# Moving columns and weights an odd number of 64 bytes apart, and the mixers of two layers merged with their projection units

## The chip, the cores and the metric

The kernel runs on one core of one Trainium2 chip. The metric is the time of one execution in microseconds on the device; lower is better. Times of before and after are medians of several runs, and one more execution is recorded by the hardware profiler.

## The reference, cut to what matters

Two stacks of layers work on one sequence of 256 tokens with 1,024 channels, in float32.

```python
def first_block(x, c, ...):                    # 2 layers
    for l in range(DEPTH):
        mod = silu(c) @ ada_w[l] + ada_b[l]    # nine vectors of shift, scale, gate
        x = x + 0.5 * gt1 * swiglu(modulate(rmsnorm(x), sh1, sc1), ffn1_w_in, ffn1_w_out)
        x = x + gt2 * mixed(...)               # attention + convolution + gated linear attention
        x = x + 0.5 * gt3 * swiglu(modulate(rmsnorm(x), sh3, sc3), ffn2_w_in, ffn2_w_out)

def second_block(x, mem, ...):                 # 4 layers
    mem_n = rmsnorm(mem, norm_mem)
    for i in range(4):
        hn = rmsnorm(x, norm_mix[i])
        mix = (diff_attention, hgrn2, chunked_sgu)[i % 3](hn, ...)
        x = x + mix
        x = x + mem_cross_attention(rmsnorm(x), mem_n, w_q, w_kv, w_o)
        x = x + swiglu(rmsnorm(x), w_gu, w_down)
    return rmsnorm(x, norm_final)

def hgrn2(h, w_in, w_out, lb, onorm_g):        # layer 1 of the second block
    q, f, i, g = split(h @ w_in, 4)
    log_f = logaddexp(log(lb), log1p(-lb) + log_sigmoid(f)); key = 1 - exp(log_f)
    # per head: o[t] = sum over s <= t of (q[t] * product of exp(log_f) over (s, t]) . key[s] * i[s]
    return (rmsnorm(o, onorm_g) * silu(g)) @ w_out

def chunked_sgu(h, w_in, w_out, vnorm_g, w_s, b_s):   # layer 2
    u, v = split(gelu(h @ w_in), 2); v = rmsnorm(v, vnorm_g)
    mixed = tril(w_s) @ v per chunk of 128 tokens and group of 128 channels, + b_s
    return (u * mixed) @ w_out
```

Layers 0 and 3 of the second block have difference attention. The memory that cross-attention reads has 256 rows.

## The kernel before, in words

**Weights.** All weights are float32 in HBM (528 MB are read in all), and those of the projections stream through four slots of the tile `raw` (128 partitions x 2,048 floats each) on SP's DMA queue. A piece that fills a slot is a unit: 256 columns of a matrix with 1,024 rows, as eight tiles of 128 rows (k). ACT rounds a unit to the type fp32r into the slot's place in `whi` (L729), and DVE writes the remainder, `raw` less `whi`, into `wlo` (L1119). Activations are kept as two parts in the same way: `hhi` and `hlo` (the normed x, by columns of 256 tokens for each k), `mhi` and `mlo` (the normed memory), `ghi` and `glo` (the feed-forward product), and `fhi` and `flo` (the two halves of `parts_f`). A product is then three matmuls in fp32r, high by high, low by high and high by low, so a unit is 8 x 2 x 3 = 48 matmuls of 256 columns on TensorE (PE). `ahead(pos)` is the call by which ACT and DVE split the weights of coming units; a unit's result lies in one PSUM bank (`u.b`), which ACT or DVE evicts.

**Orders of the matmuls.** Their functions differ in what lies between two of them:

- `product` (L1790 to L1792): for each block m of 128 output columns, for each k, the three parts; also used by `half`, one m at a time.
- token-major units (L1836 to L1838, halves L2160 to L2162): the activation is the stationary operand and the weights are the moving one.
- `both` (L1808), for units that read h, and the output stage `outp` (L2314): for each k, part by part, both m.
- `ab_wide` (L1960, L1961) in the feed-forward stages of the second block: one matmul moves 512 columns (`fhi` and `flo` of one k) past `whi`, and one of 256 moves `fhi` past `wlo`. A unit has 16 such pairs; there are 88 such units.
- `outs` (L1975, in the last step L2015): the output weights of the feed-forward stages, with `ghi` and `glo` moving, 24 matmuls per slot and step of 128 output rows.

A feed-forward step is three units' worth of work, 144 matmuls of 256 columns where it is not wide. In three of the four feed-forward stages of the first block the modulation's matrix (`ada_w`) is also loaded and multiplied.

**Addresses.** Each partition of SBUF holds the tiles one behind the other, in the order of the `sb(...)` calls. Before, a step of `PHASE` = 8 floats (32 bytes) is added behind each slot of `whi` and `wlo` and in front of each of `hlo`, `mhi`, `mlo`, `ghi`, `glo` and `parts_f`. Taken modulo 32 floats and relative to `whi`, slot s of `whi` and `wlo` begins at 8 s, `hhi` at 0, `hlo` at 8, `mhi` at 16, `mlo` at 24, `ghi` at 0, `glo` at 8, and `fhi` and `flo` at 16. An odd number of 64 bytes is 16 floats modulo 32.

**Layers with hgrn and sgu.** The order of work is that of the list `stages`, which every engine's program runs through; each engine works strictly in that order, and semaphores (`q[...]`, `read`, `used`) order engines against one another. Layer 1 has a stage `project` (12 units hq, hf, hv), a stage `tree8` (a tree of nine levels over the tokens: per level PE multiplies keys and queries of all eight heads, 32 matmuls of 128x128, L2044, DVE scales queries and keys for the next level, L1453 and L1454, and copies the level's part of the matrix out of PSUM, L1478), and a stage `hgrn_out` (4 gate units, the sums over tokens, the norm, the product with the gate). Layer 2 has `project` (4 units su, 4 units sv), then `sgu`: transposed spatial weights, the norm of v, mixed matmuls (L2269), the product with u. In both, memory's values (units xv) are projected later, ahead of cross-attention. The difference attention of layers 0 and 3 is already one stage, in which its units are laid among the heads (`DIFF_ORDER`, the first five of them, `LEAD`, ahead). Its own units take PSUM banks 0 and 1 in turn, and memory's values too. The two key units of cross-attention (xk) come ahead of the mixer's norm and take the next banks of the running count; ACT evicts them (L879). In layer 3 the banks are those of the first own units, in layer 0 they are others.

## Time and profile before

| | |
|---|---|
| median of 3 runs | 2966.79 us (2960.71 to 2968.15) |
| profiled execution | 2968.39 us, span of the records 2966.6 us |
| PE busy | 2796.0 us, 94% of the span, 21,031 matmuls |
| DVE, ACT busy | 1951.2 us (66%), 1368.4 us (46%) |
| read from HBM | 528.10 MB, 179 GB/s over the span |
| mean clock granted to PE | 0.972 of full speed |

Busy times come from the records of one execution. The record of a matmul reaches over the start of the next ones, so a mean record of 280 ns doesn't say that a matmul takes 280 ns of the engine; the time from one start to the next does. "Idle before" is the time for which an engine stood still ahead of an instruction of the group, and behind the arrow stands what ended it; "issue" is time for which the profile shows no reason. The mean clock below 1 comes from stretches in which PE has little to do.

### The profile page before, as it was taken

The page shows a single profiled execution, that of the slowest core. Times are in us where ns is not written, and L with a number is a line of the kernel's source. Part 1 is how long each engine was busy: PE and PEld are TensorE (multiplying, and loading weights), DVE is VectorE, ACT ScalarE, POOL GpSimd, SP SyncE. Part 2 cuts the span into 40 slices and gives each one's busy share as a digit, 9 for nine tenths or more (in the row PEclk, how much of TensorE's full clock was granted, in tenths as well). Part 3 has the DMA queues.
Part 4 walks back from the last instruction along what each step waited for, and adds up shares of the span by engine and source line. Part 5 has one row for each costly group of instructions (what it writes and reads, how often), then busy time and mean ns, then how long its engine had stood idle before and what let it go on. Part 6 is the DMA issues. An engine that isn't in the chain of part 4 may idle for free.

```text
span 2966.6 us, 50727 instructions
## 1 busy us (share of the span) xinstructions
PE 2796.0 (94%) x21031; PEld 2655.9 (90%) x21031; DVE 1951.2 (66%) x2718; ACT 1368.4 (46%) x1640; POOL 0.7 (0%) x5
## 2 busy tenths in 40 slices
PE   6899979999998899999999978999989999999998
PEld 5899869999998699999899978999989899999897
DVE  5887776878777655676566665566655566675665
ACT  3335434344354354555454514454544544554453
POOL 0000000000000000000000000000000000000000
PEclk8899979999999899999999999999999999999999
DMA  8987506868864145655255623445645255543453
GB/s 238 323 283 239 173 13 236 294 234 293 291 227 148 43 162 178 203 167 170 90 195 185 213 72 108 134 143 197 198 157 185 97 201 192 190 143 115 170 177 107
DMA packets 458799, 533.02 MB, mean 180 GB/s; under 512 B 9879, under 2 KB 435081, under 8 KB 458633
## 3 DMA queue, kind: packets, MB, share of 16 engines
q1 hardware_dynamic: 457340, 530.11, 53.8%
q8 instruction: 109, 1.79, 0.3%
q10 hardware_dynamic: 1293, 0.65, 0.1%
q14 instruction: 57, 0.47, 0.0%
HBM read 528.10 MB, written 2.62 MB: 179 GB/s over the span
## 4 chain that ended last, share of the span: by engine, by line
PE 85%; DVE 8%; ACT 2%; issue 2%; DMA 1%; SPq 0%; ACTq 0%; DVEq 0%
PE ps L1975 15%; PE ps L1960 11%; PE ps L1808 10%; PE ps L2314 8%; PE ps L1790 7%; PE ps L1791 6%; PE ps L1792 6%; PE ps L1961 6%; PE ps L2044 2%; PE ps L2015 2%; DVE wlo L1119 2%; DVE work L1499 1%; PE ps L1838 1%; PE ps L1836 1%; PE ps L1837 1%
## 5 line engine op out<-in xcount | busy, mean ns | idle before, releaser
L1119 DVE TENSOR_TENSOR wlo<-raw,whi 128x2048 fp32r<-128x2048 f32 (+1 forms) x514 | 976.4, 1918 | 424.9 <-ACT whi L729 421.2
L729 ACT ACTIVATE whi<-raw 128x2048 fp32r<-128x2048 f32 (+1 forms) x514 | 826.6, 1615 | 388.5 <-PE ps L1792 119.7
L1960 PE MATMUL ps<-parts_f,whi 128*128 128x512 f32 x1408 | 499.5, 397 | 10.2 <-issue 10.2
L1790 PE MATMUL ps<-hhi,whi 128*128 128x256 f32 x1488 | 426.3, 286 | 15.7 <-issue 13.0
L1791 PE MATMUL ps<-hlo,whi 128*128 128x256 f32 x1488 | 421.7, 283 | 0.0
L1792 PE MATMUL ps<-hhi,wlo 128*128 128x256 f32 x1488 | 421.6, 283 | 0.0
L1961 PE MATMUL ps<-parts_f,wlo 128*128 128x256 f32 x1408 | 397.0, 282 | 0.0
L1975 PE MATMUL ps<-glo,whi 128*128 128x256 f32 x1280 | 360.7, 282 | 0.0
L1975 PE MATMUL ps<-ghi,whi 128*128 128x256 f32 x1280 | 358.8, 280 | 1.6 <-DVE wlo L1119 1.5
L1975 PE MATMUL ps<-ghi,wlo 128*128 128x256 f32 x1280 | 359.6, 281 | 0.0
L1960 PEld LDWEIGHTS ps<-parts_f,whi 128*128 128x128 f32 x1408 | 267.2, 190 | 70.9 <-issue 11.6
L1790 PEld LDWEIGHTS ps<-hhi,whi 128*128 128x128 f32 x1488 | 283.6, 191 | 19.7 <-issue 19.6
L1791 PEld LDWEIGHTS ps<-hlo,whi 128*128 128x128 f32 x1488 | 284.3, 191 | 0.5 <-issue 0.5
L1792 PEld LDWEIGHTS ps<-hhi,wlo 128*128 128x128 f32 x1488 | 284.1, 191 | 0.0
L1961 PEld LDWEIGHTS ps<-parts_f,wlo 128*128 128x128 f32 x1408 | 267.0, 190 | 0.1
L1975 PEld LDWEIGHTS ps<-ghi,whi 128*128 128x128 f32 x1280 | 241.9, 189 | 3.8 <-issue 2.2
L1975 PEld LDWEIGHTS ps<-ghi,wlo 128*128 128x128 f32 x1280 | 240.7, 188 | 0.0
L1975 PEld LDWEIGHTS ps<-glo,whi 128*128 128x128 f32 x1280 | 240.6, 188 | 0.0
L1808 PE MATMUL ps<-hhi,whi 128*128 128x256 f32 x992 | 206.1, 290 | 20.1 <-DVE hlo L1284 16.2
L1808 PE MATMUL ps<-hlo,whi 128*128 128x256 f32 x992 | 201.4, 285 | 0.0
L1808 PE MATMUL ps<-hhi,wlo 128*128 128x256 f32 x992 | 201.3, 285 | 0.0
L1223 DVE SCALAR_TENSOR_TENSOR work<-work,silu_c 128x256 f32<-128x256 f32 x490 | 196.9, 476 | 0.0
(275 smaller groups left out, 4684.9 us busy)
## 6 DMA issues: line engine op xcount, KB each, us to landing
raw<-in_ffn_w_in SPq DMA_DIRECT2D x88, 1024.0 KB, 7.9
raw<-in_ffn_w_gu SPq DMA_DIRECT2D x88, 1024.0 KB, 5.1
work<-in_ada_w SPq DMA_DIRECT2D x72, 1024.0 KB, 8.2
raw<-in_ffn_w_out SPq DMA_DIRECT2D x88, 512.0 KB, 5.9
raw<-in_ffn_w_down SPq DMA_DIRECT2D x88, 512.0 KB, 5.6
raw<-in_ca_w_kv SPq DMA_DIRECT2D x32, 1024.0 KB, 5.7
raw<-in_mix_w_in SPq DMA_DIRECT2D x24, 1024.0 KB, 6.2
raw<-in_da_w_in SPq DMA_DIRECT2D x24, 1024.0 KB, 5.3
```

The lines of the kernel that those rows point to most:

```text
L729: f(whi[:, s, 0:size], raw[:, s, 0:size], ACT.Copy).then_inc(hi_done[s], 1)
L1119: tt(wlo[:, s, 0:size], raw[:, s, 0:size], whi[:, s, 0:size].bitcast(F32), ALU.subtract).then_inc(lo_done[s], 1)
L1223: m = stt(acc, w, silu_c[:, k:k + 1], acc, ALU.mult, ALU.add)
L1790: mm(dst, wh, xh, start=first, stop=False)
L1791: mm(dst, wh, xl, start=False, stop=False)
L1792: return mm(dst, wl, xh, start=False, stop=last)
L1808: o = mm(ps[:, slot, 256 * m:256 * m + 256], w[:, k, P * m:P * m + P], x_[:, k, :], start=k == 0 and i == 0 and m == 0, stop=k == KT - 1 a ...
L1960: mm(ps[:, banks[m], :], th[:, k, c], parts_f[:, :, k, :], start=k == 0, stop=False)
L1961: o = mm(ps[:, banks[m], 0:S], tl[:, k, c], fhi[:, k, :], start=False, stop=k == KT - 1)
L1975: o = mm(dst, a_, b_[:, t, :], start=first and t == 0 and i == 0 and m % 2 == 0, stop=False, skip_group_check=True)
L2015: o = mm(dst, a_, b_[:, t, :], start=False, stop=t == 1 and i == 2 and m % 2 == 1, skip_group_check=True)
L2314: o = mm(ps[:, bank, 256 * m:256 * m + 256], w[:, k, P * m:P * m + P], x_[:, k, :], start=k == 0 and i == 0 and m == 0, stop=k == KT - 1 a ...
```

## The change

The memory's layout, the two stages of layers 1 and 2, and the choice of banks change; the arithmetic is the same.

1. **Layout.** The steps of 8 floats are gone. `Slots` puts slot s of `whi` and `wlo` at 2,048 s + 32 (s // 2) floats. 48 floats stand ahead of `hhi`, 32 ahead of `mhi`, nothing between the others. Modulo 32 floats, all slots of `whi` and `wlo` are at 0 and all moving tensors at 16.
2. **hgrn.** One stage of 20 units in place of three stages: the 16 of before and memory's values. Five lead. The tree is cut in two half trees of four heads, one after the other, 18 half levels of 16 matmuls; behind each half level 1 or 2 halves of a unit follow (`H_FILL`), behind the last eight more. The sums over tokens, norms and gate products of the first half tree's heads are laid among the second's levels. `hv` is evicted by ACT, before by DVE. The result goes to `fhi` and `flo`, before to `hhi` and `hlo`.
3. **sgu.** One stage of 12 units: su 0, sv 0 to 3, su 1 to 3, memory's values. The spatial weights are turned behind the third, the four mixed steps stand behind units 6 to 9 (from 0). The result goes to `fhi` and `flo`.
4. **Banks.** `banks_beside(keys)` gives the first own units of the diff and hgrn stages the two banks of 0 to 3 that the key units don't use; after that two banks alternate. `st.reads` is taken behind the units, where before it was taken ahead of them.

```diff
-PHASE = 8
+class Slots:
+    def __getitem__(self, key):
+        rows, s, cols = key
+        at = UNIT * s + 32 * (s // 2)
+        return self.v[rows, at + cols.start:at + cols.stop]
...
+    def banks_beside(self, keys):
+        beside = sorted({0, 1, 2, 3} - {u.b for u in keys}, reverse=True)
+        first = 1 - beside[1] if beside[1] < 2 else 0
+        return chain(beside, cycle((first, 1 - first)))
...
-        whi = sb("whi", [P, SLOTS, UNIT + PHASE], F32R)
-        wlo = sb("wlo", [P, SLOTS, UNIT + PHASE], F32R)
+        whi = Slots(sb("whi", [P, SLOTS * UNIT + 32], F32R))
+        wlo = Slots(sb("wlo", [P, SLOTS * UNIT + 32], F32R))
         x = sb("x", [P, KT, S])
+        sb("phase_h", [P, 48])
         hhi = sb("hhi", [P, KT, S], F32R)
-        sb("phase_hlo", [P, PHASE])
         hlo = sb("hlo", [P, KT, S], F32R)
-        sb("phase_mhi", [P, PHASE])
+        sb("phase_m", [P, 32])
         mhi = sb("mhi", [P, KT, S], F32R)
-        sb("phase_mlo", [P, PHASE])
         mlo = sb("mlo", [P, KT, S], F32R)
-        sb("phase_ghi", [P, PHASE])
         ghi = sb("ghi", [P, 2, S], F32R)
-        sb("phase_glo", [P, PHASE])
         glo = sb("glo", [P, 2, S], F32R)
-        sb("phase_parts_f", [P, PHASE])
         parts_f = sb("parts_f", [P, 2, KT, S], F32R)
...
+        HGRN_ORDER = (("hq", 0, 0), ("hq", 0, 1), ("hf", 1, 0), ("hf", 1, 1), ("hq", 0, 2),
+                      ("hq", 0, 3), ("hf", 1, 2), ("hf", 1, 3), ("hv", 2, 0), ("hv", 2, 1), ("hv", 2, 2),
+                      ("hv", 2, 3), ("hgate", 3, 0), ("hgate", 3, 1), ("hgate", 3, 2), ("hxv", 4, 0),
+                      ("hgate", 3, 3), ("hxv", 4, 1), ("hxv", 4, 2), ("hxv", 4, 3))
+        H_FILL = (1, 1, 2, 1, 1, 2, 1, 1, 2, 1, 1, 1, 1, 1, 1, 1, 1, 2)
+        H_DONE = [LEAD - 1 + sum(H_FILL[:g]) // 2 for g in range(len(H_FILL) + 1)]
...
+                banks = plan.banks_beside(keys)
+                st.own = [plan.column(w, at * D, name, n, next(banks), token_major=at == 2)
+                          for name, at, n in DIFF_ORDER]
...
+        def half_tree(st, g):
+            side, L = divmod(g, LEVELS)
+            return st.tree + side, L, HALF * side
+        def half_bank(tree, h, L):
+            return 4 + 2 * ((LEVELS * tree + L) % 2) + h // 2
...
+            def hgrn(st):                       # VectorE
...
+                for g in range(2 * LEVELS):
+                    tree, L, h0 = half_tree(st, g)
...
+                    up(tree, L, hq[:, heads, :], hk[:, heads, :], hf[:, heads, :])
+                    if g:
+                        keep(g - 1)
+                        for m in range(H_DONE[g - 1], H_DONE[g]):
+                            evict(us[m + 1])
+                            ahead(us[m + 2].pos)
...
+            def sgu(st):                        # VectorE
+                for n in range(3):
+                    ahead(us[n].pos)
...
+                ahead(us[6].pos)
+                for p in range(4):
+                    ahead(us[7 + p].pos)
+                    gated(p)
+                ahead(us[11].pos)
...
+            def hgrn(st):                       # TensorE
...
+                for u, src in us[:LEAD]:
+                    unit(u, src, st.h)
+                for b in (2, 3):
+                    pe.wait_ge(read[b], st.reads[b])
+                for g, n in enumerate(H_FILL):
...
+                    pe.wait_ge(q["level_cp"], LEVELS * tree + L - 1)
+                    level(tree, L, hq, hk, HALF,
+                          lambda h, L: ps[:, half_bank(tree, h, L), 256 * (h % 2):256 * (h % 2) + 256],
+                          lambda h: (slice(0, P), h0 + h))
+                    if g == LEVELS + 2:
+                        tokens(0)
+                    if g == LEVELS + 4:
+                        pair_sum(0)
+                    if g == LEVELS + 6:
+                        tokens(1)
+                    if g == LEVELS + 8:
+                        pair_sum(1)
+                    fill(n)
+                fill(1)
+                tokens(2)
+                tokens(3)
+                fill(2)
+                pair_sum(2)
+                fill(1)
+                pair_sum(3)
+                fill(4)
...
+                for n, u in enumerate(us):      # TensorE, sgu
+                    unit(u, "h" if n < 8 else "mem", st.h)
+                    if n == 2:
+                        turn_weights()
+                    if 6 <= n <= 9:
+                        mixed(n - 6)
...
-                    hi, lo = (fhi, flo) if st.mixer.kind == "diff" else (hhi, hlo)
+                    hi, lo = (fhi, flo) if st.mixer.kind in ("diff", "hgrn", "sgu") else (hhi, hlo)
```

## Rows read from the trace of the kernel before

**Rows 1.** The page, the chain of work that ended last, by engine.
```profile
PE 85%; DVE 8%; ACT 2%; issue 2%; DMA 1%; SPq 0%; ACTq 0%; DVEq 0%
```

**Rows 2.** Windows over two feed-forward stages: length, busy us (records) of each engine, PE clock, DMA share, GB/s.
```profile
502.83:647.15 144.32, 144.32 (x1219) 144.32 (x1218) 113.94 (x177) 54.90 (x48) 0.00 (x0) 1.00 0.86 292
1085.48:1222.17 136.69, 136.69 (x1154) 136.69 (x1154) 68.00 (x66) 57.72 (x51) 0.00 (x0) 1.00 0.58 192
```

**Rows 3.** Groups of PE's matmuls by line, whole span: busy us, mean ns of a record, idle before.
```profile
L1960 PE MATMUL ps<-parts_f,whi 128*128 128x512 f32 x1408 | 499.5, 397 | 10.2 <-issue 10.2
L1790 PE MATMUL ps<-hhi,whi 128*128 128x256 f32 x1488 | 426.3, 286 | 15.7 <-issue 13.0 <-DVE wlo L1119 2.7
...
L1975 PE MATMUL ps<-glo,whi 128*128 128x256 f32 x1280 | 360.7, 282 | 0.0
...
L1808 PE MATMUL ps<-hlo,whi 128*128 128x256 f32 x992 | 201.4, 285 | 0.0
...
L2314 PE MATMUL ps<-hlo,whi 128*128 128x256 f32 x512 | 104.8, 287 | 0.0
...
L1836 PE MATMUL ps<-whi,hhi 128*128 128x256 f32 x256 | 74.0, 289 | 0.0
...
L2162 PE MATMUL ps<-whi,hlo 128*128 128x256 f32 x96 | 26.9, 280 | 0.0
```

**Rows 4.** Timeline of PE, output units of the difference-attention layers: start us, us, what.
```profile
1358.06 0.65 PE L2314 MATMUL ps<-parts_f,whi 128*128 128x256 f32 x4
...
1363.54 0.63 PE L2314 MATMUL ps<-parts_f,whi 128*128 128x256 f32 x4
...
1369.19 0.64 PE L2314 MATMUL ps<-parts_f,whi 128*128 128x256 f32 x4
...
2672.39 0.62 PE L2314 MATMUL ps<-parts_f,whi 128*128 128x256 f32 x4
...
2677.83 0.63 PE L2314 MATMUL ps<-parts_f,whi 128*128 128x256 f32 x4
```

**Rows 5.** Windows over a part of a mixing stage and over two neighbouring wide units (slots 0, 1).
```profile
320.00:370.00 50.00, 46.01 (x345) 41.62 (x343) 46.42 (x72) 25.37 (x26) 0.00 (x0) 0.98 0.46 148
2000.91:2006.54 5.63, 5.63 (x35) 4.93 (x34) 3.05 (x4) 1.58 (x2) 0.00 (x0) 1.00 0.85 298
2006.54:2012.08 5.54, 5.54 (x34) 4.87 (x33) 2.08 (x3) 3.04 (x3) 0.00 (x0) 1.00 0.26 104
```

**Rows 6.** Window over the hgrn tree and gate units.
```profile
1729.40:1829.50 100.10, 73.67 (x520) 69.23 (x519) 63.35 (x110) 21.12 (x26) 0.00 (x0) 0.91 0.17 53
```

**Rows 7.** Groups by line in that window: busy us, mean ns, idle before and releasers.
```profile
L2044 PE MATMUL ps<-work 128*128 128x128 f32 x256 | 35.1, 303 | 18.9 <-DVE work L1454 15.3 <-DVE work L1444 2.6 <-DVE work L1420 1.1
...
L1478 DVE COPY_PREDICATED work<-con,ps 128x256 f32<-128x256 int32 x56 | 19.3, 436 | 0.0
...
L1119 DVE TENSOR_TENSOR wlo<-raw,whi 128x2048 fp32r<-128x2048 f32 x4 | 9.2, 2288 | 7.0 <-ACT whi L729 7.0
L1453 DVE TENSOR_TENSOR work<-work 128x1024 f32<-128x1024 f32 x7 | 8.6, 1226 | 9.9 <-PE ps L2044 9.8
```

**Rows 8.** The chain in that window, one level of the tree: start us, us.
```profile
1745.04 3.82 PE ps L2044 x32
```

**Rows 9.** Window over the spatial gating's own work.
```profile
2194.90:2222.50 27.60, 18.45 (x134) 17.45 (x133) 14.91 (x22) 11.39 (x15) 0.00 (x0) 0.88 0.26 77
```

**Rows 10.** Timeline at the first unit of the last layer.
```profile
2546.61 0.99 DVE L1284 SCALAR_TENSOR_TENSOR hlo<-work,hhi 128x256 fp32r<-128x256 f32 x2
...
2547.88 0.77 PE L1808 MATMUL ps<-hhi,whi 128*128 128x256 f32 x2 [3.91 <-ACT work L879]
```

**Rows 11.** Window over that unit's first matmuls.
```profile
2547.80:2550.20 2.40, 2.32 (x11) 2.35 (x12) 0.74 (x1) 2.40 (x3) 0.00 (x0) 0.50 0.02 7
```

**Rows 12.** Timeline of PE, output weights in the feed-forward stage from 502 us.
```profile
502.67 0.28 PE L1975 MATMUL ps<-ghi,whi 128*128 128x256 f32 x1
...
505.59 0.28 PE L1975 MATMUL ps<-ghi,whi 128*128 128x256 f32 x1
```

More of the change, by code:

```diff
@@ L15 @@
 from contextlib import ExitStack
+from itertools import chain, cycle
 import numpy as np
@@ L451, in build @@
                 w = a["hg_w_in_2"][j]
-                units = project("hgrn", plan.columns(w, 0, 4, "hq") + plan.columns(w, D, 4, "hf")
-                                + plan.columns(w, 2 * D, 4, "hv", token_major=True))
-                tree = take("tree")
-                stages.append(Stage(kind="tree8", units=units, tree=tree))
-                gate = plan.columns(w, 3 * D, 4, "hgate")
-                last_use[0] = gate[-1]
-                stages.append(Stage(kind="hgrn_out", units=gate, last=gate[-1], tree=tree, gn=take("gn", 4)))
+                st = Stage(kind="hgrn", tree=take("tree", 2), gn=take("gn", 4))
+                banks = plan.banks_beside(keys)
+                st.own = [plan.column(*((w, at * D, name, n) if at < 4 else (wkv, D, name, n)), next(banks),
+                                      token_major=at in (2, 4)) for name, at, n in HGRN_ORDER]
+                st.reads = list(plan.reads)
+                st.units = st.own
+                st.by = {u.what: u for u in st.own}
+                last_use[0] = st.by["hgate", 3]
+                vunits = [st.by["hxv", n] for n in range(4)]
+                stages.append(st)
                 w_out = a["hg_w_out_2"][j]
@@ L461, in build @@
                 w = a["sg_w_in_2"][j]
-                units = project("sgu", plan.columns(w, 0, 4, "su") + plan.columns(w, D, 4, "sv", token_major=True))
-                stages.append(Stage(kind="sgu", units=units, last=units[-1]))
+                st = Stage(kind="sgu")
+                st.own = plan.columns(w, 0, 1, "su") + plan.columns(w, D, 4, "sv", token_major=True)
+                st.own += [plan.column(w, 0, "su", n, plan.slot) for n in (1, 2, 3)]
+                st.gates, st.inner = st.own[:1] + st.own[5:], st.own[1:5]
+                last_use[0] = st.own[-1]
+                st.mem = vunits = plan.columns(wkv, D, 4, "sxv", token_major=True)
+                st.units = st.own + st.mem
+                stages.append(st)
                 w_out = a["sg_w_out_2"][j]
@@ L477, in build @@
                                 pairs=take("pairs", 4)))
+            stages[-1].values = ([xv[:, :, 256 * h:256 * h + 256] for h in range(4)], h_xv, s_xv)[i % 3]
             ready = out_project(a["ca_w_o_2"][i])
@@ new lines, in next_unit @@
+                def next_unit(m):
+                    evict(us[m])
+                    ahead(us[m + 1].pos)
+                for u in us[:LEAD - 1]:
+                    take_out(u)
+                ahead(us[LEAD - 1].pos)
+                for m in range(LEAD - 1, 12):
+                    next_unit(m)
+                act.wait_ge(q["level_mm"], LEVELS * (st.tree + 1))
+                squares(0)
+                next_unit(12)
+                norm_root(0)
+                next_unit(13)
+                squares(1)
@@ new lines, in sgu, with next_unit, high @@
+            def sgu(st):
+                us = st.units
+                def next_unit(n):
+                    evict(us[n])
+                    ahead(us[n + 1].pos)
+                def high(p):
+                    act.wait_ge(q["sgu_v"], SG_V + 2 * p + 2)
+                    f(fhi[:, 2 * p:2 * p + 2, :], s_t[:, p % 2, :], ACT.Copy).then_inc(q["sgu_hi"], 1)
+                ahead(us[0].pos)
+                for n in range(5):
+                    next_unit(n)
+                log_exp_tables()
+                for w_, n in all_read(st.inner):
@@ L2108, in mix1 @@
                             pe.wait_ge(q["level_cp"], LEVELS * st.tree + j)
-                        level(st, j, c_q, c_k, 4, dst, part)
+                        level(st.tree, j, c_q, c_k, 4, dst, part)
                     if j == 4:
@@ L2233, in hgrn_out, with hgrn, fill, tokens @@
-            def hgrn_out(st):
-                us = st.units
-                pe.wait_ge(q["level_cp"], LEVELS * (st.tree + 1))
-                def tokens(pair):
-                    if pair > 1:
-                        pe.wait_ge(q["gn_out"], st.gn + pair - 1)
-                    for h in (2 * pair, 2 * pair + 1):
-                        o = over_tokens(ps[:, 4 + pair % 2, 256 * (h % 2):256 * (h % 2) + 256], hv,
+            def hgrn(st):
+                us = [(u, "mem" if u.what[0] == "hxv" else "h") for u in st.units]
+                values = [st.by["hv", p] for p in range(4)]
+                halves = iter([(u, src, m) for u, src in us[LEAD:] for m in range(2)])
+                def fill(n):
+                    for _ in range(n):
+                        half(*next(halves))
+                def tokens(p):
+                    pe.wait_ge(*bank_read(values[p]))
+                    pe.wait_ge(q["level_cp"], LEVELS * (st.tree + p // 2 + 1))
+                    if p == 1:
+                        pe.wait_ge(q["gn_out"], st.gn + 1)
+                    for h in (2 * p, 2 * p + 1):
+                        o = over_tokens(ps[:, (2, 2, 4, 6)[p], 256 * (h % 2):256 * (h % 2) + 256], hv,
```

263 lines of the change are left out of this document (143 added, 120 removed).

## The prediction

> **What bounds the kernel now.** I read the page first, and of it the chain of work that ended last. PE holds 85% of it, DVE 8%, DMA 1% [rows 1]. So a transfer made earlier is worth next to nothing, and two things are: the time PE takes for one matmul, and the places where it stands still. For the first, the windows over whole feed-forward stages: in the one from 1085 us PE is busy all of its 136.69 us and issues 1,152 of the 256-column matmuls (1,154 records; 8 steps of 144), so one every 118.6 ns, at full clock, with DMA at 0.58. In the stage from 502 us DMA is at 0.86 and DVE at 79%, and still PE is never idle: 144.32 us [rows 2]. Its busy records overlap (mean 280 to 290 ns each), so a matmul's price is the step from one start to the next, never the mean of a record. Then the groups of PE by line, for how many there are: L1790 to L1792 1,488 each, L1975 1,280 each of three, L1808 992 each, L2314 512 each, which make 12,816; twenty smaller groups (L1836 with 256 the first, L2162 with 96 the last) hold 3,360 more; and 1,408 pairs of a 512- and a 256-column matmul come from the wide units (L1960, L1961) [rows 3]. For the second, windows, groups and the timeline of the three stages that the edits touch [rows 6 to 12].
>
> **Part 1, the spacing of moving columns and weights.** It changes no instruction, only addresses. The trace of before has one stream in which every moving tensor already lies an odd number of 64 bytes from the weights that the array takes in beside it: the output units of the difference-attention layers whose weights are in slot 0 (fhi, flo at 16 floats modulo 32, whi and wlo of slot 0 at 0). The other three slots are 8, 16 and 24 floats on. The starts of these units' 48 matmuls tell the price: slot 0 takes 1363.54 − 1358.06 = 5.48 us, the next 1369.19 − 1363.54 = 5.65; in the last layer slot 0 takes 5.44 [rows 4], which is 113.3 ns a matmul and so 5.2 under the 118.5 that I take as the mean of all such units (the stage above gives 118.6). The first of the two begins at the old spacing and only then settles, at 0.04 us the unit.
>
> The layout after puts all four slots and all moving tensors in the position of that one stream. Which matmuls gain? Of 16,176, those of the two mixing stages of the first block stand behind DVE, which is busy 46.42 of 50 us there [rows 5]; I leave out their 26 units, 1,248, so 14,928 stay. 14,928 × 5.2 ns = **−78**; settling in half of the 311 units, 0.04 us each, **+6**. The bounds: nothing, if that stream is quick for another reason than its addresses (its order of matmuls is one of five in the kernel); or 0.0054 us each, −84, if the mean is taken from the stage and all settle at once.
>
> The wide units go the other way. The wide unit in slot 0 has odd multiples already (parts_f and slot 0) and takes 5.63 us; the one in slot 1, at 32 bytes, 5.54 [rows 5]. After, all 88 are like slot 0. If slots 1 and 3, half of them, go up by 0.09: **+4**; bounds 0 and +8 (all of them).
>
> The Trainium skill ("TensorE: Matmul & The Clock Gate", Part 2, the step on LDWEIGHTS) says that TensorE has two independent SBUF read ports and that "Loading the next tile's weights doesn't steal SBUF read bandwidth from the running matmul." By that, addresses could not matter, and the term would be 0. The trace disagrees as far as two slots of one stream differ by 3 to 4% with the same instructions [rows 4]; but it shows it for one stream alone, so the rule stays a rival below.
>
> **Part 2, hgrn in one stage.** Now the tree and the gate units take 100.10 us in which PE is busy 73.67 [rows 6]. A level is 32 matmuls in 3.82 us (0.119 each) [rows 8], then PE stands until DVE has done both products of the next level (L1453 and its like on L1454, 1.23 us each) [rows 7]. PE's own work by start steps: 4 gate units of 5.65, 22.6; 272 tree matmuls at 0.119, 32.4; 32 + 8 for tokens and sums, 32 × 0.12 + 8 × 0.24 = 5.8; 16 of the output unit, 1.9: 62.7. So 37 us are waits and half clock (the granted clock is 0.91). After, a half level is 16 matmuls (1.9 us), with one half unit (2.7) behind it in 14 of 18 levels and two in four. DVE has per half level: the two products at half size, a little over half of 1.23 each, 1.35; the small fold behind them, which I put at 0.3; four copies (L1478) at 0.44, 1.74; and 11 units' low halves (L1119) at 2.29 over 18 levels, 1.40: 4.8 us against PE's 1.9 + 22/18 × 2.7 = 5.2. PE is the longer on average, but in a level with one half unit a low half (2.29) in front of the products (1.7 with the fold) makes 4.0 against a cover of 2.7, 1.3 late; in half of the 14 such levels that is 9 us. The way in and out of the tree I put at 2. Gain 37 − 9 − 2 = **−26**; bounds −37 and, if every level is late by 1.5, 18 × 1.5 + 2 = 29, −8. The values of memory that come into this stage are the same units moved; hv's eviction goes from DVE to ACT, which is busy 21.12 of 100 us here. SP's queue gets the same transfers in the order of units; DMA is at 0.17 here, so that hides it.
>
> **Part 3, sgu among units.** 27.60 us, PE busy 18.45 [rows 9]: 9.2 idle. After, two units (11 us) lie between the last sv and the first mixed matmuls, and memory units behind each pair. The cover is a unit's 5.4 us per pair; DVE is busy 14.91 us in the whole stretch, under 3.8 for each of the four pairs even if all of it were theirs. **−9**, bounds −4.5 (half of it comes back as waits on ACT and DVE among the units) and −9.
>
> **Part 4, banks of the first units.** In the last layer PE waits 3.91 us for ACT's eviction of the keys from bank 0 (L879), which stands in order behind the norm on ACT; then the clock is 0.50 for the 2.40 us to 2550.20, which do half of their work, 1.2, and some more behind [rows 10, 11]. With another bank the units start as soon as the norm's first columns are there. **−6**, bounds −3.9 and −7. What is late next is the norm's last column: it is done at 2546.61 + 0.99 = 2547.60, and a unit begun at 2547.88 − 3.91 = 2543.97 wants it 7 × 0.68 = 4.8 later, at 2548.7. So it is not late.
>
> **Sum**, against the profiled execution, 2968.4 (span 2966.6 and 1.8 around it): 2968.4 − 78 + 6 + 4 − 26 − 9 − 6 = 2859.4. The median of the runs shown is 1.6 lower: **2858**.
>
> **The rivals.** Parts 2 to 4 alone are −41.
>
> A, the forecast: 0.47; its own range is 2835 to 2880: below by 6 (part 1 at −84), 6 (no settling) and 11 (tree at −37), above by 4 (wide at +8) and 18 (tree at −8).
>
> B, addresses do nothing on average: the stream of rows 4 is quick for its order and its place. For it: the trace has no other order at 113 ns, and the wide units are slower at that spacing. Against it: slot 1 of the same order, in the same stage, is slower. 2968.4 − 41 − 1.6 = 2926. It is also what the skill's rule of two ports would give. 0.22.
>
> C, only the order by two columns of weights for each k settles (L1808 with 2,976 and L2314 with 1,920 records, the order of the quick stream): 4,896 × 5.2 = 25; the orders of L1790, L1836 and L1975, which write one bank area until it is complete, keep their step. 2926 − 25 + 4 = 2905. 0.18.
>
> D, the forecast with a tree that gains nothing, each half level being late behind DVE's low halves and the copies: 2858 + 26 = 2884. 0.06; DVE's 4.8 against 5.2 is close.
>
> E, slower. The layout puts every unit where the worst reading of before is: the output weights of the stage at 502 us take 505.59 − 502.67 = 2.92 us for 24, 121.7 ns [rows 12]. That is 3.2 ns over the mean: 14,928 × 3.2 = +48, +4 for the wide, −41: 2968.4 + 11 − 1.6 = 2978. The sign turns where (41 − 4) / 14,928 = 2.5 ns are lost, at 121.0 ns a matmul. Against it: that unit's slot lies 8 floats from the quick position. 0.05.
>
> Some 0.02 are left for no net change, a loss of phases that eats the stages' 41.
>
> **How the numbers follow.** A measurement of this kernel tells about 0.3%, 9 us, from no change. A, B, C and D are faster, 0.93; 0.02 same and 0.05 slower, of which I move 0.01 to same for an E that is half as bad: 0.93, 0.03, 0.04. The likeliest is A: 2858. The range is to leave out 2 in 10: A's lower half reaches to 2835; above it must take in D, C and B, whose own spread is ± 5: up to 2932. That leaves E, the no change and the tails.
>
> **What would show it.** In the profile after: a plain feed-forward stage of eight steps like that from 1085 us at 8 × 144 × 113.3 ns = 130.5 us instead of 136.7 (B: 136.7 still; C: 136.7 there, while units of L1808 take 5.44 us; E: 140); every output unit (L2314) at 5.44 to 5.48 us in all four slots; wide units of all slots at 5.63. The hgrn tree with 18 levels at 5.2 us of PE, and idle time of L2044 for DVE under 10 us in place of 18.9; over 25 would be D. In sgu no idle time of PE over 1 us in front of the mixed matmuls; no wait for L879 in front of the first unit of the last layer. The prediction is wrong if the cause of the quick stream is not the distance of moving data from weights, if DVE's or ACT's operand reads slow as their own addresses move, or if the quick step only lasts for streams without a neighbour.

## The result, and the profile after

The kernel after takes 2872.46 us (median of 4 runs, 2870.35 to 2875.08); before takes 2967.38 (4 runs, 2960.71 to 2968.15). The ratio is 0.9685, 95% interval 0.9668 to 0.9702: 94.9 us quicker. The forecast was 2858, so 109 quicker. Five later runs of the same kernel gave 2873.47.

The page of the profiled execution (2870.35 us, span 2868.6), the chain of work that ended last, by engine. It answers to [rows 1]:

```profile
PE 83%; DVE 9%; ACT 3%; issue 3%; DMA 2%; SPq 1%; ACTq 0%; DVEq 0%
```

PE still holds the chain, with a little less of it: its matmuls have become shorter, the waits of the other engines mostly have not. Then windows over the stretches that answer to [rows 2, 5, 6, 9] (length, busy us and records of each engine, clock of PE, DMA share, GB/s): eight steps of the second and of the last feed-forward stage of the first block, the ten steps of its first one up to the last outputs, two wide units in one stage and two in the next, the merged hgrn stage from the tree's first level to its output, the merged sgu stage, and one token-major unit:

```profile
500.78:639.55 138.77, 138.77 (x1218) 138.77 (x1218) 112.09 (x176) 55.67 (x48) 0.00 (x0) 1.00 0.92 299
1066.37:1197.19 130.82, 130.82 (x1154) 130.82 (x1154) 68.01 (x66) 57.69 (x51) 0.00 (x0) 1.00 0.60 197
96.26:275.22 178.96, 170.63 (x1435) 169.99 (x1434) 149.18 (x254) 66.01 (x58) 0.00 (x0) 0.95 0.89 290
1461.25:1472.54 11.29, 11.29 (x67) 9.88 (x65) 6.91 (x7) 4.62 (x5) 0.00 (x0) 1.00 0.75 258
1937.53:1948.62 11.09, 11.09 (x66) 9.77 (x65) 5.23 (x7) 4.62 (x5) 0.00 (x0) 1.00 0.61 209
1662.72:1792.29 129.57, 121.76 (x996) 118.16 (x994) 89.31 (x149) 59.49 (x58) 0.00 (x0) 0.99 0.34 108
2077.16:2161.68 84.52, 83.58 (x718) 83.28 (x717) 57.18 (x57) 48.28 (x53) 0.00 (x0) 1.00 0.62 198
1232.84:1238.51 5.67, 5.67 (x51) 5.67 (x50) 4.37 (x2) 2.40 (x2) 0.00 (x0) 1.00 1.09 360
```

The reader is to see, line by line: the stage that took 136.69 us takes 130.82 (130.5 was forecast), with the same 1,152 matmuls, so 113.6 ns for each; the one with DMA at 0.86 took 144.32, takes 138.77 and has DMA at 0.92, still without an idle moment of PE. In the first feed-forward stage PE idles 8.3 us. A wide unit takes 11.29 / 2 = 5.65 us in the one stage and 5.55 in the other. The merged stages keep PE busy for 94 and 99% of their time. The last line is a unit of the token-major order: 5.67 us for 48 matmuls, no quicker than before (117.9 ns a matmul on average).

The timeline of PE at the first three output units of layer 0, and the start of the fourth (start us, us, what), answers to [rows 4]:

```profile
1332.53 0.71 PE L2472 MATMUL ps<-parts_f,whi 128*128 128x256 f32 x4 [0.99 <-DVE work L1507]
...
1338.13 0.62 PE L2472 MATMUL ps<-parts_f,whi 128*128 128x256 f32 x4
...
1343.57 0.62 PE L2472 MATMUL ps<-parts_f,whi 128*128 128x256 f32 x4
...
1349.01 0.62 PE L2472 MATMUL ps<-parts_f,whi 128*128 128x256 f32 x4
```

The second and third slot now take 5.44 us as the first did in the last layer before; the first one, 5.60, has a wait of 1 us in front and settles.

Where the time went, from the start of the first matmul of each stretch in the traces of four kernels (us; the two in the middle are the first two experiments):

| stretch | before | layout alone | structure alone | after |
|---|---|---|---|---|
| start, to the first output weights | 93.8 | 95.5 | 93.7 | 96.3 |
| first feed-forward stage | 183.5 | 184.4 | 183.0 | 186.2 |
| the other three of the first block | 517.7 | 496.7 | 517.6 | 496.9 |
| mixing stages and their outputs | 348.3 | 339.8 | 349.3 | 340.5 |
| layer 0, difference attention | 122.9 | 121.5 | 124.0 | 122.6 |
| layer 1, mixer to the end of cross-attention | 279.1 | 273.7 | 249.9 | 246.9 |
| layer 2, the same | 173.4 | 170.3 | 161.5 | 158.7 |
| layer 3, difference attention | 129.4 | 127.8 | 123.0 | 120.9 |
| four wide feed-forward stages | 658.9 | 650.9 | 658.9 | 650.4 |
| the rest, up to the last of these | 444.6 | 435.4 | 444.4 | 434.6 |
| sum | 2951.6 | 2895.9 | 2905.3 | 2853.7 |

### The profile page after: what moved, and what is told of

Its sections match the earlier page's. It is cut to its first block, busy times and chain, and to the rows that moved or that the text cites. A ratio compares the mean times of both kernels' runs of the same rounds, so it can differ in the third digit from the quotient of the medians.

```text
span 2868.6 us, 50786 instructions
## 1 busy us (share of the span) xinstructions
PE 2717.4 (95%) x21031; PEld 2579.0 (90%) x21031; DVE 1940.6 (68%) x2727; ACT 1389.5 (48%) x1664; POOL 0.7 (0%) x5
## 4 chain that ended last, share of the span: by engine, by line
PE 83%; DVE 9%; ACT 3%; issue 3%; DMA 2%; SPq 1%; ACTq 0%; DVEq 0%
PE ps L2097 14%; PE ps L2082 11%; PE ps L1930 9%; PE ps L2472 7%; PE ps L1912 7%; PE ps L1913 6%; PE ps L1914 6%; PE ps L2083 6%; DVE wlo L1206 2%; PE ps L2137 2%; DMA work<-in_ada_w 2%; DVE work L1586 2%; PE ps L2166 1%; PE ps L2282 1%; PE ps L2284 1%
## 5 line engine op out<-in xcount | busy, mean ns | idle before, releaser
L2082 PE MATMUL ps<-parts_f,whi 128*128 128x512 f32 x1408 | 497.7, 396 | 11.9 <-issue 11.9
L1912 PEld LDWEIGHTS ps<-hhi,whi 128*128 128x128 f32 x1600 | 303.7, 190 | 21.0 <-issue 21.0
L1913 PEld LDWEIGHTS ps<-hlo,whi 128*128 128x128 f32 x1600 | 303.8, 190 | 0.7 <-issue 0.7
L1914 PEld LDWEIGHTS ps<-hhi,wlo 128*128 128x128 f32 x1600 | 303.3, 190 | 0.0
```

The lines of the kernel that those rows point to most:

```text
L1912: mm(dst, wh, xh, start=first, stop=False)
L1913: mm(dst, wh, xl, start=False, stop=False)
L1914: return mm(dst, wl, xh, start=False, stop=last)
L2082: mm(ps[:, banks[m], :], th[:, k, c], parts_f[:, :, k, :], start=k == 0, stop=False)
```

## The experiments

Steps are given below as the time from one start to the next, 48 matmuls a unit, by unit from the traces. "Moving less whi" is the distance in floats of the tensor that moves from the slot's high part, modulo 64; in the kernel after it is 48 for h in slots 0 and 1 and 16 in slots 2 and 3, and the other way round for all other moving tensors. wlo lies 32 from whi. A unit is called quick if its mean step, past its first matmuls, is under 114.5 ns. Of `product`, the units that read h are counted (101, before 94); 16 more read the memory.

**Layout alone, structure alone.**

The first is the kernel before with this edit; the second is the kernel after with the same edit undone.

```diff
-        whi = sb("whi", [P, SLOTS, UNIT + PHASE], F32R)
-        wlo = sb("wlo", [P, SLOTS, UNIT + PHASE], F32R)
+        whi = Slots(sb("whi", [P, SLOTS * UNIT + 32], F32R))
+        wlo = Slots(sb("wlo", [P, SLOTS * UNIT + 32], F32R))
         x = sb("x", [P, KT, S])
+        sb("phase_h", [P, 48])
         hhi = sb("hhi", [P, KT, S], F32R)
-        sb("phase_hlo", [P, PHASE])
...
```

> The kernel before with the new addresses and nothing else. Theory 1 (addresses set the step of a matmul, and the parts add up): column-major units at 113.3 ns, token-major units at 117.8 as in the profile after, so about 13,800 matmuls outside the mixing stages gain 4 to 5 ns, less what the first feed-forward stage can't use because its transfers bound it: 55 to 65 us, 2902 to 2912. Theory 2 (the step came from something in the new order of work, as a busier PE): units stay at 118 to 119 ns, within 10 us of 2967.

> The kernel after with the addresses of before: merged hgrn and sgu stages and the choice of banks. Theory 1 (parts add up): what is left of 95 us when the addresses give 55 to 65, so 30 to 40 us under 2967, 2927 to 2937, and my sum of the three parts said 41. Theory 2: 2870 to 2880. First feed-forward stage of before, 183.5 us, without the two waits of 2.5 and 4.1 us for wlo. If those waits stay with the old addresses, they belong to the execution, not to the quicker PE.

Measured: 2914.79 (4 runs, ratio 0.9828, 0.9811 to 0.9845) and 2923.81 (0.9849, 0.9831 to 0.9867), beside 2967.66. So 52.9 and 43.8 us; their sum is 96.7, the whole change 94.9. The parts add up, and theory 1 holds, with the layout 2 us under and the structure 4 us over the gain that I gave as the nearest end. In the layout's run every group of column-major units goes from 117.4 to 119.0 ns on average to between 113.4 and 115.6, the 38 token-major units stay (117.9, 117.7), the wide pairs too (349.7, 350.1). The first feed-forward stage takes 183 to 186 us in all four kernels.

**The roles of the two positions.**

```diff
 raw = sb("raw", [P, SLOTS, UNIT])
+sb("phase_w", [P, 16])
 whi = Slots(sb("whi", [P, SLOTS * UNIT + 32], F32R))
...
-sb("phase_h", [P, 48])
+sb("phase_h", [P, 16])
```

> The kernel after with all of whi and wlo moved to 16 floats modulo 32 and all activations to 0: the same distances, the roles of the two positions exchanged. If only the distance counts: column-major units 113.3 ns, token-major ones 117.8, time 2870 to 2875. If it counts which position the stationary operand has (at 0 quick, at 16 slow): column-major units go to 117.8 (+60 us) and token-major ones to 113.3.

Measured: 2878.48 us, one run. Most column-major units stay at 113.3, token-major ones at 117.7: the position of either one doesn't count, the distance does. But this layout also turns each 48 into a 16 and back, and that shows. The wide pairs exchange: 353 ns in slots 0 and 1, 347 in 2 and 3. And of the units of `product` and the output weights, 68 of 101 and 110 of 160 are at 113.3, in the kernel after 95 of 101 and 148 of 159; the rest are near 119, all in slots where moving less whi is 16.

**No step between the slots.**

```diff
-        at = UNIT * s + 32 * (s // 2)
+        at = UNIT * s
```

> The kernel after without the 32 floats between slots 1 and 2 of whi and wlo: modulo 64 all slots of whi are at 0 and all of wlo at 32. In the profile after the wide units take 347 ns a pair in slots 0 and 1 and 353 in slots 2 and 3, which differ only by those 32 floats. If the step of a wide pair follows the position modulo 64 of whi and wlo against fhi: all at 347, 44 units x 16 pairs x 6 ns = 4.2 us quicker, 2868. Rival (slots 2 and 3 are slower for another reason, such as the transfers that land beside): no change, or a loss in the 113.3 ns of the other units, whose slots then all lie alike modulo 64.

Measured: 2885.81 (5 runs, 0.9724, 0.9711 to 0.9737). The wide pairs came as the theory had it, the time did not: the rival's loss came as well. Windows over two units of `product`, the two of output weights behind them, and two wide units:

```profile
1063.54:1074.43 10.89, 10.89 (x99) 10.89 (x97) 4.21 (x3) 6.76 (x7) 0.00 (x0) 1.00 0.57 197
1074.43:1080.13 5.70, 5.70 (x50) 5.70 (x49) 4.11 (x3) 2.98 (x2) 0.00 (x0) 1.00 0.60 186
1471.60:1482.69 11.09, 11.09 (x67) 9.76 (x65) 6.39 (x7) 4.62 (x5) 0.00 (x0) 1.00 0.73 251
```

The wide units are all quick (11.09 for two). The output weights take 5.70 us for 48 matmuls in place of 5.46, 155 of 159 units near 119.1, though ghi lies 16 from whi as in slots 0 and 1 of the kernel after, where most were quick.

**All at 16 over whi.**

```diff
-        at = UNIT * s + 32 * (s // 2)
+        at = UNIT * s
...
-        sb("phase_h", [P, 48])
+        sb("phase_h", [P, 16])
...
-        sb("phase_m", [P, 32])
```

> The kernel after with no step between slots and every moving tensor (hhi, hlo, mhi, mlo, ghi, glo, fhi, flo) at 16 floats modulo 64 beside whi at 0 and wlo at 32; in the run without the slots' step hhi was at 48. That run had wide pairs at 347 ns in all slots, but the output weights of the feed-forward stages at 119.1 in place of 113.3. Theory (a stream keeps the step that it comes with, and it falls back where the sign of the distance changes between the stream before, hhi at 48, and ghi at 16): with one sign everywhere the output weights are at 113.3 and the wide pairs at 347, so 4.2 us quicker than the kernel after, 2868. Rival (equal positions modulo 64 of all slots make the output weights slow): 119.1 stays for them, 2881 to 2889 as without the slots' step.

Measured: 2890.97 (5 runs, 0.9744, 0.9722 to 0.9767). The theory is wrong as I put it: one sign everywhere was not enough. The same three windows:

```profile
1064.23:1075.64 11.41, 11.41 (x98) 11.41 (x97) 5.41 (x5) 6.76 (x7) 0.00 (x0) 1.00 0.59 188
1075.64:1081.35 5.71, 5.71 (x51) 5.71 (x49) 4.12 (x3) 2.98 (x2) 0.00 (x0) 1.00 0.56 185
1476.95:1488.04 11.09, 11.09 (x67) 9.77 (x66) 6.81 (x7) 4.62 (x5) 0.00 (x0) 1.00 0.79 264
```

Now much of `product` is slow as well (11.41 for these two units), with 47 of 101 units at 113.3; of the output weights 35 of 160 are. Moved from 48 to 16, in slots 0 and 1, it lost what it had. The units of `both` and of the output stages read from the same place and keep 113.3 (50 of 55, 38 of 40).

**Whi and wlo alike.**

```diff
-        at = UNIT * s + 32 * (s // 2)
+        at = UNIT * s
...
-        whi = Slots(sb("whi", [P, SLOTS * UNIT + 32], F32R))
+        whi = Slots(sb("whi", [P, SLOTS * UNIT + 64], F32R))
...
-        sb("phase_m", [P, 32])
```

> As the run with one sign everywhere, but wlo at 0 modulo 64 as whi, so that the two tensors that a token-major unit moves in turn lie alike modulo 64. Theory 3 (token-major units stay at 117.8 because their moving tensors th, tl, th alternate between 0 and 32, where column-major ones move xh, xl, xh that lie alike): token-major units go to 113.3, the whole gains 1,824 x 4.5 ns = 8 us at most. Rival (it is the order, in which one activation is the weight for two matmuls of different moving tensors): 117.8 stays. Column-major units: 113.3 if odd multiples of 64 bytes are all that counts.

Measured: 2916.65, one run. Theory 3 holds in part, and the other half of the expectation falls. Windows over two units of `both`, over one token-major unit and over two wide units:

```profile
1246.76:1258.07 11.31, 11.31 (x99) 11.31 (x97) 9.30 (x14) 8.96 (x11) 0.00 (x0) 1.00 0.46 142
1258.07:1263.52 5.45, 5.45 (x50) 5.45 (x49) 3.76 (x2) 2.41 (x2) 0.00 (x0) 1.00 1.10 359
2002.81:2014.13 11.32, 11.32 (x67) 9.85 (x66) 5.13 (x6) 4.62 (x5) 0.00 (x0) 1.00 0.55 192
```

The token-major unit takes 5.45 us, with DMA at its busiest, and 21 of the 38 do; in every other layout none does. The column-major ones fall back: 11.31 for two, and 6 of 55, 4 of 101 and 2 of 160 units are left at 113.3, though every distance is an odd multiple of 64 bytes. The wide pairs, too, are at 353 ns in all four slots (11.32 us for two units), though fhi lies 16 over whi as in all_plus, where they took 347. So the distance from whi alone doesn't settle the step; where wlo lies counts as well.

**Other distances.**

```diff
-        sb("phase_h", [P, 48])
+        sb("phase_h", [P, 64])                 # h at 0
...
-        sb("phase_m", [P, 32])
+        sb("phase_m", [P, 8])                  # m at 8
...
+        sb("phase_g", [P, 16])                 # g at 24
...
+        sb("phase_f", [P, 16])                 # f at 8 (modulo 32)
```

> The kernel after with other distances of the moving tensors from whi, in floats modulo 32: hhi and hlo 0, mhi and mlo 8, ghi and glo 24, fhi and flo 8. If only 16 is quick: units of h (both, product, output stage) at 117.8 or more, those of the memory, the feed-forward output weights and the units that read fhi too, and the time is that of the run with the old addresses, 2924, or over it. If 8 and 24 are quick too: those groups at 113.3 and only the units of h slow.

Measured: 2923.55, one run: at 0, 8 and 24 nothing is quick. No unit of any order is at 113.3; h at 0 gives 118.9, g at 24 gives 119.4, m at 8 gives 118.3, f at 8 in the output stage 117.7. The same two windows, of `both` and of a token-major unit:

```profile
1245.00:1256.37 11.37, 11.37 (x99) 11.37 (x97) 9.36 (x14) 8.96 (x11) 0.00 (x0) 1.00 0.46 142
1256.37:1262.09 5.72, 5.72 (x50) 5.72 (x49) 3.70 (x2) 2.40 (x2) 0.00 (x0) 1.00 1.10 357
```

**The layout that these point to.** For column-major streams 48, for the wide pairs 16, and wlo 32 from whi in every slot.

```diff
-        at = UNIT * s + 32 * (s // 2)
+        at = UNIT * s
...
-        sb("phase_m", [P, 32])
...
+        sb("phase_f", [P, 32])
         parts_f = sb("parts_f", [P, 2, KT, S], F32R)
```

> The kernel after, unchanged, to stand beside the two below on the same chip: 2870 to 2875.

> The kernel after with one sign: whi at 0 and wlo at 32 floats modulo 64 in all slots, hhi, hlo, mhi, mlo, ghi and glo at 48, fhi and flo at 16. Rule read from the five layouts run: with moving less whi at 48 modulo 64 column-major streams are at 113.3 ns always, at 16 they are at 113.3 or 119 by what came before; a wide pair takes 347 at 16 and 353 at 48. So all column-major units at 113.3, every output weight too, all wide pairs at 347, token-major units 117.8. Each feed-forward stage of the second block then takes 161.6 us, where two of four take 163.6 in the kernel after: 4 us quicker, and 2 to 3 more from outs at 115.2 in slot 1: 2865 to 2869. Rival (the positions of the slots against each other matter, since both layouts without their step had slow units): outs near 119 again, 2880 to 2890.

Measured, side by side: 2873.47 for the kernel after (2867.68 to 2881.95) and 2863.12 for this one (2861.45 to 2868.17; 0.9660, 0.9645 to 0.9675), five runs each: 10.4 us between the medians, with one run of each crossing. The three windows again:

```profile
1051.79:1062.67 10.88, 10.88 (x99) 10.88 (x97) 4.99 (x4) 6.76 (x7) 0.00 (x0) 1.00 0.58 195
1062.67:1068.11 5.44, 5.44 (x51) 5.44 (x49) 3.92 (x3) 2.99 (x2) 0.00 (x0) 1.00 0.59 193
1456.65:1467.73 11.08, 11.08 (x66) 9.75 (x65) 6.50 (x7) 4.61 (x5) 0.00 (x0) 1.00 0.75 256
```

All three are quick at once: 100 of 101 units of `product`, 158 of 159 of output weights (some of these at 114.1 ns), and the wide pairs at 347.1 ns on average. The rival, that the slots must differ from one another, falls. What the addresses explain is smaller than the 10 us: the four wide stages take 647.7 us in place of 650.9, the three others of the first block 495.4 against 496.9. The profiled executions, 2881.95 and 2862.84, are further apart than the medians, and most of what is left lies in their mixing stages, which without their outputs take 146 to 154 us each over the traces of all kernels, and differ by up to 6 us between two executions of the kernel after; so 4 to 5 us of the 10 are the layout's, and what the rest is stays open.

**The banks of the difference attention.**

```diff
-                st.own = [plan.column(w, at * D, name, n, next(banks), token_major=at == 2)
-                          for name, at, n in DIFF_ORDER]
+                st.own = [plan.column(w, at * D, name, n, turn % 2, token_major=at == 2)
+                          for turn, (name, at, n) in enumerate(DIFF_ORDER)]
```

> The kernel after with the banks of before for the difference attention (0 and 1 in turn). My step said 6 us in the last layer: its stage from 120.9 to about 127.5 us, with the wait for L879's successor back; and layer 0, where the keys lie in other banks, from 122.6 back to 121.5, as the two runs without the new banks had it. Net 5 to 6 us slower than the kernel after. Rival (the last layer's gain came from the merged stages ahead of it): the stage stays at 121.

Measured: 2877.81, one run. The last layer's stage takes 127.2 us in place of 120.9, layer 0's 121.4 in place of 122.6. Who PE waited for in the last layer's stage:

```profile
PE ps L1929 <- ACT work L927: 4.4, 1, 4.4
```

This one wait is back; the kernel after has none there. The window over the 4.00 us behind it:

```profile
2464.66:2468.66 4.00, 4.00 (x21) 4.00 (x22) 2.42 (x2) 3.83 (x3) 0.00 (x0) 0.57 0.01 4
```

The mean clock is 0.57, close to the lower level of 0.50, so some 1.7 us of work at full clock are lost there. The gain of 6.3 is this and the wait of 4.4, as forecast.

> The kernel with one sign and, in layer 0 alone, banks 0 and 1 in turn from the first own unit on, as before: layer 0's stage at 121.5 in place of 122.6, so 1.1 us quicker than the kernel with one sign, 2864 to 2868; if the 1.1 us of layer 0 were a spread of executions, no difference.

```diff
-                banks = plan.banks_beside(keys)
+                banks = plan.banks_beside(keys) if i else cycle((0, 1))
```

Measured: 2865.29 (5 runs, 2862.87 to 2866.39), no different from 2863.12. In its trace layer 0's stage does take 121.0 us in place of 122.2; 1.1 us is less than the runs can tell.

**More work for VectorE in the tree.**

```diff
                     if g:
+                        dve.wait_ge(q["level_cp"], LEVELS * st.tree + g - 1)
+                        tt(gate_w[:, :, :], ..., ALU.mult)      # 128x512
+                        tt(cs[:, :, :], ..., ALU.mult)          # 128x512
                         keep(g - 1)
```

> The kernel after with two more products of 128x512 on VectorE in front of each copy out of a half level (17 levels, 2 x 0.69 us; results are not used). My reckoning was 4.8 us of VectorE against 5.2 of TensorE in a half level; with 1.4 more VectorE is the longer one by 1.0, so 17 us or more, 2888. Rival (the units among the levels hide much more than I reckoned): under 3 us, 2871 to 2876.

Measured: 2866.19, one run: not slower than the kernel after, whose nine runs go from 2867.68 to 2881.95. The window over its hgrn stage, and below it who PE waited for there (total us, times, longest):

```profile
1658.20:1787.82 129.62, 121.86 (x993) 118.28 (x993) 108.01 (x182) 59.49 (x58) 0.00 (x0) 0.99 0.34 107
```

```profile
PE ps L2169 <- DVE work L1541: 5.0, 5, 2.1
PE ps L2169 <- DVE work L1531: 3.1, 2, 1.7
```

VectorE is busy 108.01 us in place of 89.31, the stage is as long (129.62, 129.57), and PE's waits are 8.1 us. The same view of the kernel after:

```profile
PE ps L2166 <- DVE work L1541: 4.7, 5, 2.1
PE ps L2166 <- DVE work L1531: 3.1, 2, 1.7
```

The rival holds: 1.1 us more in each half level are hidden, so my 4.8 us of VectorE in a half level were too many. Where the room was, the low halves of weights in the stage (1660 to 1785 us) show, first in the kernel after, then here:

```profile
L1206 DVE TENSOR_TENSOR wlo<-raw,whi 128x2048 fp32r<-128x2048 f32 x13 | 29.8, 2292 | 30.9 <-ACT whi L774 30.9
L1206 DVE TENSOR_TENSOR wlo<-raw,whi 128x2048 fp32r<-128x2048 f32 x13 | 29.8, 2291 | 16.3 <-ACT whi L774 16.3
```

VectorE stood idle for 30.9 us in front of them, until ACT had made the high halves; with the extra products it is 16.3.

## Why the prediction was right

**The forecast came as A.** Layout 52.9 us where the steps of part 1 gave 68; structure 43.8 where parts 2 to 4 gave 41. B (no effect of addresses, −41) and C (only the order by two columns, 2905) fall by layout_only: `product` and the output weights settle as `both` does. D falls by structure_only, in which layer 1 gains 29 us, and E: no group of units of the kernel after is on average over 117.8.

**Part 1, the step that failed: which matmuls gain.** The price of 5.2 ns was near (118.6 to 113.7 for `product` and the output weights, 4.9 with what does not settle). The count of 14,928 was not right. It holds 1,536 token-major matmuls outside the mixing stages, which gain nothing (8 us), and the 1,440 of the first feed-forward stage (7.5 us). 11,952 × 4.9 ns is 58.6. The runs say 46 to 56 by the ratio's interval; in the table the layout's column is 55.7 under before, 58.3 without the start and the first stage, which came out 2.6 longer. Of that, 8.5 lie in the mixing stages, more than the 384 matmuls of their outputs that I had counted can give (1.9), so part of it is the spread of those stages, and the others are some 7 short of the count. (The bound of −84 was worked out wrongly, too: 14,928 × 5.4 ns is 81.) The wide term was wrong in its mechanism: slot 0 of before was taken for the position of all, and I worked modulo 32. It goes modulo 64. Two slots went to 353 and two to 347, 349.7 to 350.2 on average, +0.7 in place of +4. The same holds for the rule as a whole, and here I had luck. "An odd number of 64 bytes" is true of five more layouts, one_sign, swapped, no_slot_step, all_plus and hi_lo_even, and these take 2863 to 2917 us. The quick stream of [rows 4] lay at 48 modulo 64, and the kernel after puts the moving tensors at 48 or 16 by slot, which happened to leave most units quick. The place of tensors against weights sets the step, as forecast; which places do it, the forecast had only in part. The token-major order stands in [rows 3] as L1836 and L2162, and one quick stream was carried over to an order that moves the weights.

**The first feed-forward stage.** Its 10 steps could not take what PE offered. Who waited there, from the waits of the kernel after (total us, times, longest):

```profile
ACT whi L774 <- DMA raw<-in_ffn_w_in: 24.9, 9, 7.8
...
DVE work L1307 <- DMA work<-in_ada_w: 13.1, 5, 2.8
...
PE ps L2097 <- DVE wlo L1206: 6.4, 3, 3.8
```

DMA is at 0.89 over the stage, ACT waits for weights, DVE for the modulation's matrix, and PE, in the end, 6.4 us for the low halves; before it was 1.5. The same waits with the structure alone and with the layout alone:

```profile
PE ps L2101 <- DVE wlo L1210: 1.3, 2, 0.7
PE ps L1983 <- DVE wlo L1127: 6.2, 3, 3.1
```

They are 3.8 to 8.1 us in all eleven traces of layouts with quick units, and 3.0 in offsets, where none is quick. So they belong to the quicker PE more than to the execution, which is what the expectation of structure_only asked, but not all of them do. In front of the longest of these waits in the kernel after, VectorE works through ten products of the modulation and the tables of the rotation one behind another:

```profile
209.75 3.97 DVE work L1310 x10
...
215.07 0.44 DVE cs L1261
...
216.65 1.24 DVE wlo L1206
217.88 0.14 issue
218.02 5.46 PE ps L2097 x24
```

A faster PE runs into this. [rows 2] showed DMA at 0.86 in another such stage, with no idle moment of PE; that one had the room, and I took it for all. That the transfers or VectorE's queue hold it is read from these waits; no run took one of them away.

**Part 2.** −26 was forecast; layer 1 gains 29.2 in the structure's run (279.1 to 249.9). The waits of the half levels are 7.8 us where I had 9, at seven levels as I had it: five wait for their two products and two for the single product of a tree's second level (L1531), for 0.9 and 1.6 us on average. In front of each of the seven a unit's low half stands in VectorE's order, as I had reckoned. The longest of them:

```profile
1679.64 2.29 DVE L1206 TENSOR_TENSOR wlo<-raw,whi 128x2048 fp32r<-128x2048 f32 x1 [0.54 <-ACT whi L774]
1681.85 0.69 DVE L1540 TENSOR_TENSOR work<-work 128x512 f32<-128x512 f32 x1
1682.45 0.69 DVE L1541 TENSOR_TENSOR work<-work 128x512 f32<-128x512 f32 x1
...
1683.29 0.35 PE L2166 MATMUL ps<-work 128*128 128x128 f32 x1 [2.08 <-DVE work L1541]
```

What I had not seen is why it is late: it waits for ACT's high half, in front of all seven. That is why 18.7 us more work on VectorE leave the waits as they are. The load was the wrong step: it is 89.31 of 129.57 us, 69%, not 4.8 of 5.2, for I charged the products and the masked copies to all 18 half levels, and four of these have no such products (14 of each) and four no masked copies (56 in all). [rows 7] had this in it: 56 copies over nine levels of eight heads, not 72, and seven of the products.

**Part 3.** −9 was forecast, 11.9 came (173.4 to 161.5). I counted the idle time of the window alone. Behind a wait of 5.0 us for VectorE (L1723) in it the clock is at the lower level:

```profile
2206.00:2210.00 4.00, 2.92 (x14) 2.95 (x15) 1.77 (x4) 0.00 (x0) 0.00 (x0) 0.50 0.00 0
```

The output stage gained 3.5 us; 2.8 of them are waits of its first unit for VectorE (L1743), which the window's 9.2 us of idle time held already.

**Part 4.** −6 for the last layer was right (6.4), and 1.1 us of loss in layer 0 was not foreseen: the first units' banks changed there too, without need. Both are in the table and in diff_banks_old, which is one run.

**The skill's rule.** The Trainium skill ("TensorE: Matmul & The Clock Gate", Part 2, on LDWEIGHTS) has two independent SBUF read ports, so that loading weights takes no bandwidth from the running matmul. By that, as the forecast used it, addresses could not matter. The runs disagree: layout_only changes nothing but addresses, and 56 of 62 units of `both` and 89 of 94 of `product` become quick. Without a term for the layout the change would have been 44 us (structure_only); it is 95. That it is the loading of weights that costs the running matmul its time is not shown; the runs show only that the two streams' places against each other count.

## What to carry to other kernels

Where matmuls follow each other with new weights each time, the place of the moving tensor against the weights can set some 4% of a matmul's step (1.8% of this kernel's time): read the start-to-start step of one stream by slot before believing that PE is at its limit, and try the distances modulo 256 bytes, for each order of matmuls by itself. A price found in one order holds for that order; count only the instructions of orders in which it was seen, and ask of each stage whether the other engines can feed a PE that is 5% quicker. A serial chain between levels is best hidden under units that already wait to be done, and VectorE's whole load there says little; what stands ahead of the next product in its queue, and what that waits for, does.

## What the runs showed of the hardware

All of it for fp32r matmuls of 128x128 weights by 256 columns, at full clock, with new weights for each. A stream has steady steps, 113.3 ns or one between 117 and 122, and can have either at the same distances: in all_plus 47 of 101 units of one order are at 113.3 and the rest near 119. Which one it takes depends on the distance of moving tensors and weights modulo 256 bytes and, at some distances, on something more, perhaps what came before; no run isolates it. With moving tensors 48 floats over the high weights modulo 64 and low weights 32 beyond those, every column-major order is at 113.3, apart from output weights at 114.1 in some units; at 16 `product` and the output weights take either, `both` the quick one; at 0, 8 and 24 (modulo 32) none is quick. With high and low weights alike modulo 64, column-major orders mostly lose it, and the token-major order, which moves the weights, gets it in 21 of 38 units. A pair of 512 and 256 moving columns takes 347 ns at 16 and 353 at 48, the other sign from that of the 256-column orders, as long as the low weights lie 32 beyond the high ones; with both alike it takes 353 at 16. It isn't bound to odd multiples of 64 bytes: in the kernel before, slots 1 and 3, where the distances are 40 and 24, were at 347 too. Exchanging which of the two tensors lies on the round address (here with 16 and 48 exchanged too) leaves `both`, the output stages and the token-major order as they were. Which part of the memory meets which was not found, and a layout in which both kinds of order are quick was not tried.
